# A hybrid decoder step on one core: the RMS norm taken out of the way of x, and the prompt's queries projected turned

## What is computed

```
def rmsnorm(x, g):
    y = xf * lax.rsqrt(jnp.mean(xf * xf, axis=-1, keepdims=True) + EPS)
    return (y * g).astype(x.dtype)

h = rmsnorm(x, ln_g) @ w_in                     # 3352 columns
q_n, kv_c, kv_s, kv_w, g_n, z_n, q_r, k_r, v_r, z_r, q_m, z_m = split_cols(h)
```

## Time and profile before

| | us |
|---|---|
| median of 3 runs | 971.1 (970.6 to 972.13) |
| span of the profiled execution, first to last instruction | 970.0 |
| PE busy | 928.3 |
| DVE busy | 517.3 |
| ACT busy | 382.5 |
| POOL busy | 289.1 |

### The profile page before, as it was taken

The page is one execution under the profiler, slowest core; times in us unless marked ns, Lnnn a source line. Parts: engine busy times, 40 slices in busy tenths (PEclk is TensorE's granted clock), DMA queues, the critical chain, the costliest instruction groups (busy, mean ns, idle before and its releaser), DMA issues.

```text
span 970.0 us, 20909 instructions
## 1 busy us (share of the span) xinstructions
PE 928.3 (96%) x7997; PEld 843.0 (87%) x7997; DVE 517.3 (53%) x1216; ACT 382.5 (39%) x973; POOL 289.1 (30%) x493
## 2 busy tenths in 40 slices
PE   4999999999999999999999999999999999999997
PEld 4999999999999999999988788878878888778885
DVE  6675322322222444337546677676777758944443
ACT  6333221224211012212456565656665657832221
POOL 0222222211216353462153153315311535310000
PEclk9999999999999999999999999999999999999998
DMA  7664404224242533322966156714504132424331
GB/s 242 157 218 117 158 20 170 84 100 118 69 142 83 134 127 100 104 82 60 226 191 146 36 155 240 240 44 123 167 2 126 56 103 73 134 98 134 132 133 69
DMA packets 97878, 119.16 MB, mean 123 GB/s; under 512 B 37763, under 2 KB 79779, under 8 KB 97203
## 3 DMA queue, kind: packets, MB, share of 16 engines
q1 hardware_dynamic: 84498, 74.41, 26.8%
q0 software_dynamic: 10224, 36.20, 11.0%
q10 hardware_dynamic: 3056, 7.21, 2.1%
HBM read 92.72 MB, written 32.02 MB: 129 GB/s over the span
## 4 chain that ended last, share of the span: by engine, by line
PE 78%; DVE 8%; issue 4%; DMA 4%; ACT 2%; POOL 2%; SPq 2%; DVEq 0%; ACTq 0%
PE psum L541 9%; PE psum L542 9%; PE psum L543 9%; PE psum L1727 7%; PE psum L1602 5%; PE psum L1575 3%; PE psum L1746 3%; PE psum L1747 3%; PE psum L1748 3%; PE psum L1576 3%; PE psum L770 2%; PE psum L772 2%; PE psum L771 2%; PE psum L753 2%; DMA r_rt<-in_c_rope 2%
## 5 line engine op out<-in xcount | busy, mean ns | idle before, releaser
L541 PE MATMUL psum<-a_whi,f_xhi 128*128 128x256 f32 (+1 forms) x864 | 250.9, 290 | 8.1 <-DVE f_xlo L959 4.4
L542 PE MATMUL psum<-a_wlo,f_xhi 128*128 128x256 f32 (+1 forms) x864 | 245.1, 284 | 0.0
L543 PE MATMUL psum<-a_whi,f_xlo 128*128 128x256 f32 (+1 forms) x864 | 244.3, 283 | 0.0
L541 PEld LDWEIGHTS psum<-a_whi,f_xhi 128*128 128x128 f32 x864 | 164.1, 190 | 11.9 <-issue 3.1
L543 PEld LDWEIGHTS psum<-a_whi,f_xlo 128*128 128x128 f32 x864 | 164.1, 190 | 0.0
L542 PEld LDWEIGHTS psum<-a_wlo,f_xhi 128*128 128x128 f32 x864 | 164.0, 190 | 0.0
L1907 DVE TENSOR_REDUCE p_nb<-psum 128x1 f32<-128x640 f32 (+7 forms) x224 | 110.4, 522 | 48.8 <-PE psum L1576 46.8
L1839 ACT ACTIVATE p_P<-psum,p_nb 128x640 f32<-128x640 f32 (+7 forms) x224 | 124.3, 562 | 25.9 <-DVE p_nb L1907 23.5
L685 POOL DMA_DIRECT2D h_scratch<-a_hst x117 | 64.1, 550 | 234.7 <-DVE a_hst L1015 146.4
L1602 PE MATMUL psum<-f_ident,p_P 128*128 128x128 f32 x656 | 101.8, 279 | 3.0 <-ACT p_qd L1852 1.4
L1602 PEld LDWEIGHTS psum<-f_ident,p_P 128*128 128x128 f32 x656 | 74.0, 140 | 8.6 <-ACT p_qd L1852 1.9
(11 more groups left out here) (317 smaller groups left out, 1836.6 us busy)
## 6 DMA issues: line engine op xcount, KB each, us to landing
a_wraw<-in_w_in SPq DMA_DIRECT2D x24, 512.0 KB, 4.9
h_scratch<-a_hst POOLq DMA_DIRECT2D x96, 128.0 KB, 2.6
s_SG<-in_cache_nsa_slc SPq DMA_DIRECT2D x64, 128.0 KB, 2.3
a_xraw<-in_x_prompt SPq DMA_DIRECT2D x8, 512.0 KB, 3.7
p_qd<-h_scratch SPq DMA_DIRECT2D x16, 256.0 KB, 4.0
s_MK<-in_cache_mem SPq DMA_DIRECT2D x8, 512.0 KB, 9.8
s_WG<-in_cache_nsa_win SPq DMA_DIRECT2D x8, 512.0 KB, 4.7
mix_scratch<-p_zt POOLq DMA_DIRECT2D x8, 512.0 KB, 3.8
```

What stands on the lines that cost most here:

```text
L541: nc.tensor.matmul(out, hi, wh, start=first, stop=False)
L542: nc.tensor.matmul(out, hi, wl, start=False, stop=False)
L543: return nc.tensor.matmul(out, lo, wh, start=False, stop=last)
```

## The change

Both halves touch the projection part and the queries' way:

1. **Norm.** x is transposed as it was loaded. The gain, one number for each feature, is brought onto the partitions by one small transpose (`gcol`) and multiplied into the weights during their split: four ACT operations and four DVE operations for each half of a chunk, each with a column of `gcol` as scale. The root (`rstd(t)`, one number for each row) is applied in the evictions. Steps `ss` (square, sum) and `rs` (root, inverse) stand behind the high and low parts of the tile. The first job is cut in two halves of k, and PE waits for half a chunk of weights at a time. A load of x waits for the transposes and the square sum of the tile before in its buffer.
2. **Queries.** The chunks with queries (columns 0 to 511 and q_m) are projected turned for the prompt: 128 weight columns are the loaded operand and 256 tokens stream, so the result has features on its partitions. It is multiplied by `rrow`, the root of every token times SCALE, broadcast over the partitions, which PE makes by 8 transposes in step `rrow`. The result goes to a scratch `qD` (768 rows of 1024 tokens); `load_q` reads it in pieces of 512 B into both halves of the partitions. Transposes and copies of queries in both parts fall away. Chunks 7 and 11 change places, so that all query chunks come after `rrow`.

```
-CHUNKS = [..., (1, 0, 256), (0, 0, 256), (1, 256, 256), (0, 256, 256), (0, 2840, 256), (0, 1304, 256), ...]
+CHUNKS = [..., (1, 0, 256), (0, 1304, 256), (1, 256, 256), (0, 256, 256), (0, 2840, 256), (0, 0, 256), ...]
-    ACT_CHUNKS = (5, 11, 12, 13, 14)
+    ACT_CHUNKS = (5, 7, 12, 13, 14)
+    Q_CHUNKS = (11, 9, 10)
+        steps.extend([("x", 0), ("split", ("w", 0)), ("hl", 0)])
+        steps.extend([("job_a", 0), ("x", 1), ("job_b", 0), ("ss", 0), ("hl", 1), ("ss", 1)])
+        for n in range(2, NT + 2):
             steps.append(("x", n))
             if n == 2:
                 steps.append(("split", ("w", 1)))
+            steps.extend([("hl", n), ("rs", n - 2), ("ss", n)])
...
+            if e[0] == "w":
+                for k in range(4):
+                    nc.scalar.activation(hi[:, k], raw[:, k], ACT.Copy, scale=split_gain(e, 4 * half + k)).then_inc(S("w_hi"), 1)
...
+                    ins = nc.vector.scalar_tensor_tensor(out=lo[:, k], in0=raw[:, k], scalar=split_gain(e, 4 * half + k), in1=hi[:, k].bitcast(F32), op0=ALU.mult, op1=ALU.subtract)
...
+    def mm3_turned(out, j, k, t, first, last):
+        c, tok = turned_parts(j, t)
+        wh, wl = whi[j % 2][:, k, c:c + 128], wlo[j % 2][:, k, c:c + 128]
+        hi, lo = xhi[:, k, tok:tok + 256], xlo[:, k, tok:tok + 256]
+        nc.tensor.matmul(out, wh, hi, start=first, stop=False)
+        nc.tensor.matmul(out, wl, hi, start=False, stop=False)
+        return nc.tensor.matmul(out, wh, lo, start=False, stop=last)
...
         def load_x(n):
             if n >= 2:
-                sp.wait_ge(S("x_scaled"), n - 1)
+                sp.wait_ge(S("x_tr"), 2 * (n - 1))
+                sp.wait_ge(S("x_ss"), n - 1)
...
-        pool.wait_ge(S("x_scaled"), 3)
+        pool.wait_ge(S("x_tr"), 6)
         pool.dma_start(pD[:, :, 0:1], io["page_table"]...
...
-            sp.dma_start(qd[par[i]][:, 0:8, j, :], hD[rows, 0:512]...
-            sp.dma_start(qd[par[i]][:, 8:12, j, :], hD[rows, C_QM:C_QM + 256]...
+            sp.dma_start(qd[par[i]][64 * j:64 * j + 64], qD[:, 128 * i:128 * i + 128].rearrange("(h d) t -> d h t", d=HD)).then_inc(S(f"p_q{par[i]}"), 16)
...
+            elif what == "rrow":
+                for t in range(QT):
+                    l = nc.tensor.transpose(bank(4 + t // 4)[:, 128 * (t % 4):128 * (t % 4) + 128], rstd(t).to_broadcast([128, 128]), ident[:])
...
-                nc.vector.tensor_copy(hst[n % HST][0:tile_rows(t), 0:w_n[j]], job_out(n)).then_inc(S("h_evac_dve"), 1)
+                if turned(j, t):
+                    nc.vector.tensor_tensor(dst, job_out(n), rrow[:, tok:tok + 256], ALU.mult).then_inc(S("h_evac_dve"), 1)
+                else:
+                    nc.vector.tensor_scalar(dst, job_out(n), rstd(t), None, ALU.mult).then_inc(S("h_evac_dve"), 1)
...
-            copied = kind in ("p", "q", "mk", "mt", "kt", "st")
+            copied = kind in ("p", "mk", "mt", "kt", "st")
...
             for k, part in q_at.get(v, []):
-                add(("q", k, part))
+                steps.append(("q", (k, part)))
```

More of the change, by code:

```diff
@@ L199, in build @@
     xraw = [ra(f"xraw{i}", [128, D]) for i in range(2)]
-    xs = [ra(f"xs{i}", [128, D]) for i in range(2)]
-    gb = ra("gb", [128, 2, D])
+    graw = ra("graw", [2 * KT, 128])
     x_end = ra.at
@@ L386, in build, with turned, turned_parts @@
     irows = lambda u: 128 if u < NDB // 2 else 64
-    ACT_CHUNKS = (5, 11, 12, 13, 14)
+    ACT_CHUNKS = (5, 7, 12, 13, 14)
     MEM_CHUNKS = (6, 8)
+    Q_CHUNKS = (11, 9, 10)
+    def turned(j, t):
+        return j in Q_CHUNKS and t < QT
+    def turned_parts(j, t):
+        return 128 * (t // 4), 256 * (t % 4)
     def trunk():
@@ L406, in evict @@
                 steps.append(("ev", late.pop(0)))
-        for n in range(NT + 2):
+        steps.extend([("x", 0), ("split", ("w", 0)), ("hl", 0)])
+        jobs.append((0, 0))
+        late.append(0)
+        steps.extend([("job_a", 0), ("x", 1), ("job_b", 0), ("ss", 0), ("hl", 1), ("ss", 1)])
+        for n in range(2, NT + 2):
             steps.append(("x", n))
@@ L825, in pe_trunk @@
                 r_states((6, 7)).then_inc(S("r_use"), 1)
-            elif what == "qtr":
-                pe.wait_ge(S("p_q0"), 64)
-                pe.wait_ge(S("p_klo"), 8)
-                for j in range(4):
-                    l = nc.tensor.transpose(bank(5 + n)[:, 128 * j:128 * j + 128], qd[0][:, 4 * n + j], ident[:])
-                l.then_inc(S("q0_tr"), 1)
             elif what == "ktr":
@@ L882, in act_trunk @@
                 hi(n)
-            elif what == "x_end":
-                hi(NT + 1)
+            elif what == "rrow":
+                act.wait_ge(S("c_kv"), kv_count(NIDX - 1))
+                for g in range(2):
+                    act.wait_ge(S("rrow_tr"), g + 1)
+                    nc.scalar.activation(rrow[:, 512 * g:512 * g + 512], bank(4 + g), ACT.Copy, scale=SCALE).then_inc(S("rrow"), 1)
             elif what == "split":
@@ L942, in act_trunk @@
             elif what == "qtr":
-                act.wait_ge(S("q0_tr"), n + 1)
+                act.wait_ge(S("p_q0"), 32)
                 act.wait_ge(S("w_split"), 2 * len(ring))
-                nc.scalar.activation(QA[0][:, 4 * n:4 * n + 4, :], bank(5 + n).rearrange("p (j c) -> p j c", j=4), ACT.Copy, scale=SCALE).then_inc(S("q0_hi"), 1)
+                nc.scalar.copy(QA[0][:, 4 * n:4 * n + 4, :], qd[0][:, 4 * n:4 * n + 4, :]).then_inc(S("q0_hi"), 1)
             elif what == "ktr":
@@ L1849, in act_attend @@
                     nc.scalar.copy(split_dst(n, False), split_src(n)).then_inc(S("p_shi"), 1)
-                elif kind[0] == "q" and chunk_act(n):
-                    act.wait_ge(S("p_tr"), n + 1)
-                    nc.scalar.activation(q_raw(n), bank(4 + n % 3), ACT.Copy, scale=SCALE).then_inc(S("pt_act"), 1)
                 elif chunk_act(n):
@@ L2133, in pool_attend @@
         for what, n in p_steps:
-            if what == "t" and p_chunks[n][0] == "q":
-                _, i, part = p_chunks[n]
+            if what == "q":
+                i, part = n
                 split = 3 * q_rank[i] + part + 1
-                wait_chunk_read(pool, n)
+                pool.wait_ge(S(f"p_q{par[i]}"), 32 * (rank[i] + 1))
                 if prev[i] is not None:
```

171 lines of the change are left out of this document (101 added, 70 removed).

## The result

Over nine runs of each kernel, run in turn on the same chip, the changed kernel takes 964.5 us (959.2 to 969.5) and the kernel before 970.6 (969.9 to 972.1). The ratio is 0.9933, 95% interval 0.9916 to 0.9949: by it the changed kernel is 6.5 us faster, where 15.0 were forecast. The profiled execution has a span of 962.6 us and a mean clock of 0.991; before it was 970.0 and 0.996. Two things stand out already here: the runs of the changed kernel spread over 1%, those of before over 0.2%, and the spread goes with the clock (the five runs at 0.991 or less are 964.5 to 969.5, the four above it 959.2 to 962.4).

The account below looks back on a forecast made before the run. TensorE, busy 928.3 of 970.0 us, was taken as the bound: 970.0 - 10.5 - 0.7 - 1.2 + 0.8 + 0.5 - 5.0 = 953.9, plus 1.1 unrealised and 1.1 around the span, 956.1 us; range 948 to 964 (0.85).

Parts of the forecast that it names:

- Part 1: Query transposes removed: -10.5 us for 21 groups in attention, -0.7 waiting, -1.2 in projection, +0.8 for added transposes; net -11.6.
- The 1.1 us kept back as not realised: Attention part: a tenth of what goes there, added back for places where PE is not the bound.
- rival (b): Attention part held by DVE and ACT together; half of 11.2 us lost in place of a tenth: 961 us, chance 0.12.
- Rival (d): Turned queries load late, holding GpSimd's queue so DVE and PE wait; three loads 3 us late: 965 us, chance 0.05.
- Part 3: The start: first half job at 10.7 us, x4 landing at 28.5, x5 at 35.2 in place of 40.21; -5.0 us.
- rival (a): The start: x4, then x5, land late in the page table's write, taking back the gain: 961 us, chance 0.15.
- The bound from the one load of 11.4 us: The start: x4 landing 11.4 us after issue, at 33.4; PE loses 5 us more and the start gives 0.
- The end of part 3: Last x tile: its high part moves ahead of the jobs; PE's wait there, about 1 us, gone or not; priced 0.
- Part 2: Weight splits with gain, four operations per half: 0 under PE's jobs, except at the start and near 461 us; +0.5 us.
- the estimate beside it: Weight splits, from the Trainium skill: 3.2 us a chunk on ACT, 0.3 more at each of two uncovered places; time 956.7.
- The table loads of chunk 7: Chunk 7, now gated: ACT alternates SiLU and GELU, about four more table loads of 1.28 us; 0, at most 5.
- The wait forecast near 461 us: Weight split that DVE begins late: about +1 us for the longer split, -0.5 as PE may start after the first half.

Follow-up runs that it names:

- both, write late: Changed kernel with the page-table write moved to x tile 5 and its read to tile 7: 959.2 us, 0.9889; on another chip 957.0 us, 0.9847.
- turned alone: Kernel before with only the turned queries; x, its norm and the weight split as before: 958.9 us, 0.9881.
- norm alone: Changed kernel with the queries projected and transposed as before: 971.0 us, 0.9999.
- best (end reordered): Changed kernel with last two roots and page-table write later, tile 2's squares earlier, later splits in two jobs, evictions before roots, GpSimd's copies last: 949.6 us, 0.9787.
- The late roots: Changed kernel with the last two reciprocal roots of x moved behind the third chunk's weight split: 961.4 us, 0.9902.
- whole splits: Changed kernel with each weight half split in one operation and its gain left out: 960.3 us, 0.9891.
- the kernel before with the write late: Kernel before with only the page-table write moved to x tile 5 and its read to tile 7: 969.3 us, 0.9986.

## Why the prediction was wrong

The marks, in us, each row from one profiled execution (that of "both, write late" is the fastest of its four); the middle columns are the starts of DVE's splits:

| kernel | last x tile | chunk 3 | chunk 12 | chunk 13 | first maximum | span |
|---|---|---|---|---|---|---|
| before | 72.0 | 104.6 | 383.6 | 413.4 | 492.6 | 970.0 |
| after | 73.2 | 110.8 | 390.3 | 422.3 | 498.9 | 962.6 |
| turned alone | 73.9 | 106.5 | 384.2 | 414.0 | 491.9 | 956.9 |
| norm alone | 69.1 | 106.6 | 384.7 | 414.1 | 492.0 | 969.0 |
| both, write late | 66.0 | 102.7 | 382.5 | 414.5 | 491.1 | 954.9 |
| best (end reordered) | 65.5 | 96.8 | 377.4 | 406.9 | 483.5 | 949.7 |

The changed kernel is behind the one before by 1.2, 6.2, 6.7, 8.9 and 6.3 us at the five marks, and 7.4 ahead at the end. Against the forecast the projection part is 11.2 us too long (+6.3 for -4.9) and the attention part 3.6 too short (-13.7 for -10.1), so the two errors partly cancel; the miss would have been larger without the second.

**Part 1, right, and 2 to 4 us too small.** The stretch between the first and the last row maximum, before and with the turned queries alone (length, then busy time and instructions of PE, PEld, DVE, ACT, POOL):

```profile
492.60:852.20 359.60, 347.13 (x3525) 294.00 (x3526) 261.64 (x609) 229.01 (x667) 134.85 (x239) 1.00 0.41 122
```

```profile
491.90:839.50 347.60, 336.31 (x3441) 286.53 (x3442) 247.23 (x599) 229.85 (x656) 135.64 (x239) 1.00 0.43 126
```

There are exactly 84 fewer matmuls, the 21 groups of the earlier trace rows. PE's busy time goes down by 10.8 us (for -10.5) and its idle time, 12.5 us, by 1.2 (for -0.7). The 1.1 us kept back as not realised was not lost; rival (b) did not come. ACT's share did not grow by 6 us but by 1 (256.4 to 257.6 from the first maximum on), DVE's fell by 15 (310.9 to 296.0). The matmuls of the turned projection cost nothing extra: with the turned queries alone the distance from chunk 3's split to chunk 12's is 277.7 us, before 279.0. Rival (d) did not come either, although the loads of queries take 7.6 us to land.

**Part 3, the step that failed first.** "-5.0 us" rests on "I put x4's landing at 28.5"; measured at the last x tile, the start gave +1.2. The first half job came at 11.39 (forecast 10.7). Tile 4 came at 32.73, so tile 5 stood at 41.4 instead of 35.2 and the last tile at 73.2 instead of 67. This is rival (a), for which I had given 0.15: one load in the page-table write. That it was the write, the run with the late write shows: tile 5 at 34.2, the last tile at 66.0, both a microsecond better than forecast. The write began at 19.4 us and not at 17, since PE transposed tile 2 later, it was through at 31.0 and not at 28, and the load came out 1.8 us behind it. The bound from the one load of 11.4 us was the nearer row. And I had not carried the stop on into the clock: 4.7 us of waiting is followed by 4.3 at half speed, and I had seen such a stretch in the earlier trace rows. The 4.2 us from 28.5 to 32.73 and these 2.2 lost make up the slip of tile 5, 6.2 us.

**The end of part 3, priced at 0.** "Gone or not, about 1 us; 0." From the last x tile's transposes to chunk 3's split it takes 37.6 us, before 32.6: +5.0. What I did not list is that the change moves the roots of two tiles, 12 small DVE operations, ahead of a split that has no cover; I had not counted every instruction that the moved steps bring there. The late roots give 3.2 us back, whole splits 2.3, the reordered end all of it (31.3 us).

**Part 2, right where there is cover, wrong at the edge of it.** The pieces cost what was forecast: eight in 3.28 us on DVE (2.6 to 3.3), 3.30 on ACT (2.9 in the sum, 3.2 by the estimate beside it). From chunk 3's split to chunk 12's it takes 279.5 us, before 279.0, so 3.3 us under a cover of 11.6 are free. The table loads of chunk 7 were free as well. The wait forecast near 461 us (+0.5) is not there: PE starts after the first half. The costs that came instead are where POOL worked beside DVE: the root of 2.14 us at 78 us, the pieces' 5.63 us near 390, and 4.81 once the roots are moved. With whole splits and no gain the kernel is 4 us faster. I charged nothing for POOL, though the trace of before had it: the same split took 3.87 us for two halves beside POOL's copy, where elsewhere it mostly took 2.36 (POOL's and DVE's row, kernel before):

```profile
74.32 2.03 POOL L695 COPY c_G<-c_G 128x1024 f32<-128x1024 f32 x2
```

```profile
74.70 3.87 DVE L530 TENSOR_TENSOR a_wlo<-a_wraw,a_whi 128x1024 fp32r<-128x1024 f32 x2
```

**What stays open.** With the write early the parts miss their sum by 5 us, with the write late by 3 to 7 (against the kernel before with the write late: 14.2 and 2.4 alone, 9.4 or 13.5 together). One piece of it is placed: the eviction's wait of 2.6 us, which exists only where turned jobs with DVE evictions meet pieces beside the rope (chunk 12 to 13: 32.0 us with both, 29.8 before, 29.8 and 29.4 with one part). The rest is of the size by which the same program differs between two chips. Nor do I know why the write ended at 27.5 us in the profile of the norm alone and at 31 with both, with the same instructions up to there; this is the 4.1 us between the two at the last x tile, with the clock. Whether the lower clock of the slower runs comes from such a wait could not be seen, since each profile has one execution.

## What to carry to other kernels

Where an engine's lead is spent on loads, look at what the other queues have in flight at that time: moving one transfer of 2 KB in small pieces was worth 4 us to the kernel with the turned queries, while the new norm path alone was worth nothing with that transfer early and 2.4 us with it late. A split, a root or a copy that costs nothing under eleven microseconds of cover has its price at the two or three places without cover; list these first, and every instruction that the change puts ahead of them on their engine. Price a wait of a few microseconds on TensorE with the half-speed stretch that may follow: here 2.2 and 2.7 us behind waits of 4.7 and 4.0, and nothing behind one of 2.6.

## What the runs showed of the hardware

A page-table write of 2 KB, 4 bytes at a time from GpSimd's queue, slows a load of 512 KB from SyncE's queue if they overlap. The load of x tile 4 took 8.2 us to land when issued in the middle of the write, 12 us from issue to use when issued at its start, and 3.6 with the write out of the way (median before: 3.7). Within the window from 19 to 30 us of the changed kernel, its 31 packets (queue 0) held the 16 DMA engines for more time than the 1.16 MB of the loads (queue 1):

```profile
q0 software_dynamic: 31, 0.00, 41.9%
q1 hardware_dynamic: 696, 1.16, 37.2%
```

That share does not explain the whole delay. From 24 to 28 us, with the load of tile 4 issued at 24.4, the write's packets take next to nothing, yet only 0.09 MB of the load move, in 21 packets that take 30.3% of the engines' time; what held them is not shown. From 28 us on it shares some 300 GB/s with two loads of the compression weights, issued right behind it.

```profile
q1 hardware_dynamic: 21, 0.09, 30.3%
q0 software_dynamic: 10, 0.00, 0.1%
```

VectorE's operations with two inputs from SBUF stretch beside GpSimd's work on SBUF: the square of one column (a product of the column with itself) took 2.14 us in place of 0.16 beside two copies of 2.03 us in all, eight pieces of a split 5.63 and 4.81 in place of 3.25, and with the copy moved away 3.24 again, as the run with the reordered end shows. The Trainium skill (SBUF — State Buffer, Who interferes with whom) states that a DVE instruction with two SBUF inputs contends with a GpSimd instruction that reads SBUF, and that the port pair which the two share is an exclusive lock. That the 2.14 us end within 0.1 us of the copies agrees with a wait for the other; it lasted for both copies (1.05 us each), not for one.
